# Linear-attention steps, weight splits and evictions at the block ends of the projection in a hybrid decoder step

## The reference, cut to what matters

```python
h = rms_norm(x, g_norm)
z = einsum('btd,dn->btn', h, w_in)              # all mixers' inputs and gates
ya = fox_attention(...) * silu(ga)              # forgetting attention
a_logit = einsum('btr,rk->btk', lrb, w_gla_up) + b_gla
log_a = log_sigmoid(a_logit) / GLA_TAU
ob, gla_new = gla_chunked(qb, kb, vb, log_a, gla_state)   # gated linear attention
yb = rms_norm(ob, g_gla) * silu(gb)
yc = bc * short_conv(cc * xc) * silu(gc)
merged = sum over the three of sigmoid(mg[i]) * (y_i @ w_branch_i)
out = x + merged @ w_out;  y = rms_norm(out, g_final)
```

## Time and profile before

| | us |
|---|---|
| Median of 3 executions (4195.01 to 4203.75) | 4199.2 |
| The profiled execution's own time | 4200.65 |
| Its span | 4198.8 |
| PE busy in the span | 3777.5 (90%) |
| DVE, ACT, POOL busy | 1787.0, 1705.8, 1082.0 |
| PE idle before L895, ended by DVE prj_att | 68.4 (11 times) |

### The profile page before, as it was taken

How to read it: one execution, slowest core, us unless ns; L and a number is a source line. 1 busy time by engine, 2 the same in 40 slices (tenths; PEclk the granted TensorE clock), 3 DMA queues, 4 the chain that set the end, 5 groups by cost and what they waited for, 6 DMA issues and landing times. The chain is left out here.

```text
span 4198.8 us, 60616 instructions
## 1 busy us (share of the span) xinstructions
PE 3777.5 (90%) x19285; PEld 3081.9 (73%) x19285; DVE 1787.0 (43%) x2968; ACT 1705.8 (41%) x3497; POOL 1082.0 (26%) x927
## 2 busy tenths in 40 slices
PE   7999999989999989996999993799898999599999
PEld 6787777767777778775877873577777777378887
DVE  3233433222134433232434443576666666554432
ACT  3224423435224424432443441466666666131222
POOL 0011222120011221211000000166666666622200
PEclk9999999999999999997999996899999999699999
DMA  4233333233233233324010002688888888454422
GB/s 142 92 106 110 116 131 128 87 112 116 90 110 116 98 132 130 117 82 123 1 41 11 1 11 66 211 290 287 279 283 276 289 292 277 147 214 166 157 105 82
DMA packets 356189, 590.18 MB, mean 141 GB/s; under 512 B 44953, under 2 KB 91137, under 8 KB 355974
## 3 DMA queue, kind: packets, MB, share of 16 engines
q1 hardware_dynamic: 349998, 580.21, 41.3%
q10 hardware_dynamic: 5408, 5.12, 0.4%
q0 software_dynamic: 576, 2.10, 0.2%
HBM read 475.38 MB, written 111.97 MB: 140 GB/s over the span
## 5 line engine op out<-in xcount | busy, mean ns | idle before, releaser
L854 PE MATMUL prj_z_ps<-prj_w_hi,prj_h_hi 128*128 128x512 f32 x2312 | 937.7, 406 | 15.3 <-DMA prj_bias_b<-in_b_gla_dram 9.4
L855 PE MATMUL prj_z_ps<-prj_w_lo,prj_h_hi 128*128 128x512 f32 x2312 | 913.2, 395 | 0.0
L856 PE MATMUL prj_z_ps<-prj_w_hi,prj_h_lo 128*128 128x512 f32 x2312 | 913.1, 395 | 0.0
L1800 POOL TENSOR_TENSOR sa_v_lo<-sa_v_raw,sa_v_hi 128x1024 fp32r<-128x1024 f32 x256 | 603.7, 2381 | 379.2 <-DVE sa_v_hi L1956 379.2
L854 PEld LDWEIGHTS prj_z_ps<-prj_w_hi,prj_h_hi 128*128 128x128 f32 x2312 | 443.8, 192 | 106.5 <-DVE prj_w_lo L678 9.9
L856 PEld LDWEIGHTS prj_z_ps<-prj_w_hi,prj_h_lo 128*128 128x128 f32 x2312 | 441.6, 191 | 96.7
L855 PEld LDWEIGHTS prj_z_ps<-prj_w_lo,prj_h_hi 128*128 128x128 f32 x2312 | 443.0, 192 | 87.1
L1944 DVE TENSOR_TENSOR sa_kT_lo<-sa_t_ps,sa_kT_hi 128x512 fp32r<-128x512 f32 x512 | 352.1, 690 | 252.5 <-ACT sa_kT_hi L1832 249.4
L1832 ACT CAST sa_kT_hi<-sa_t_ps 128x512 fp32r<-128x512 f32 x512 | 297.3, 584 | 239.0 <-PE sa_t_ps L2036 183.9
L678 DVE TENSOR_TENSOR prj_w_lo<-prj_w_raw,prj_w_hi 128x512 fp32r<-128x512 f32 x274 | 187.3, 703 | 408.6 <-ACT prj_w_hi L556 407.9
L2036 PE MATMUL sa_t_ps<-sa_ident,sa_k_raw 128*128 128x128 f32 x2048 | 305.8, 285 | 55.0 <-DVE sa_kT_lo L1944 54.1
(11 more groups left out here) (303 smaller groups left out, 6029.1 us busy)
## 6 DMA issues: line engine op xcount, KB each, us to landing
sa_k_raw<-in_cache_k_dram SPq DMA_DIRECT2D x512, 256.0 KB, 3.7
sa_v_raw<-in_cache_v_dram SPq DMA_DIRECT2D x512, 256.0 KB, 4.1
prj_w_raw<-in_w_main_dram SPq DMA_DIRECT2D x272, 256.0 KB, 3.2
z_scratch<-prj_z_sb SPq DMA_DIRECT2D x272, 256.0 KB
mo_mg<-z_scratch SPq DMA_DIRECT2D x51, 512.0 KB, 4.4
prj_cu<-extp_scratch SPq DMA_DIRECT2D x48, 256.0 KB
pa_raw<-z_scratch SPq DMA_DIRECT2D x12, 1024.0 KB, 10.9
prj_x_in<-in_x_all_dram SPq DMA_DIRECT2D x17, 512.0 KB, 3.8
```

The lines of the kernel that those rows point to most:

```text
L854: pe.matmul(out, h_hi[:, slot_of(t), k], hi, start=(k == 0), stop=False)
L855: pe.matmul(out, h_hi[:, slot_of(t), k], lo, start=False, stop=False)
L856: mm = pe.matmul(out, h_lo[:, slot_of(t), k], hi, start=False, stop=(k == KC - 1))
L1800: pool.tensor_tensor(v_lo[:, slot, part], v_raw[:, slot, part], v_hi[:, slot, part].bitcast(F32), ALU.subtract).then_inc(vlo_ready, 1)
```

## The change

At a block end ACT and DVE now run `gla_steps(u)` first, then all eight splits; `evict(u)` is put off to the next unit, behind that unit's `gla_steps`. SP issues the eight loads of a block end before the unit's store. There are six raw buffers in place of four; to make room, `junk` (the unused output of the square) becomes bf16. The waits for the gates' weights (`up_loaded`) and for DVE's zero fills move from before the first unit to the linear attention's own steps.

```diff
-    W_RING, RAW, Z_RING, PS_RING = 9, 4, 4, 3
+    W_RING, RAW, Z_RING, PS_RING = 9, 6, 4, 3
-        junk = m.sb("junk", [P, D_MODEL])
+        junk = m.sb("junk", [P, D_MODEL], BF16)
 # SP, at every unit
-                for s in BEFORE.get(u, []):
+                for s in BEFORE.get(u, []) + AFTER.get(u, []):
                     load_w(s + RAW)
                 store(u)
-                for s in AFTER.get(u, []):
-                    load_w(s + RAW)
 # ACT, gla step 1
+                    act.wait_ge(up_loaded, 32)
+                    act.wait_ge(gla_filled, GLA_FILLED)
 # ACT, before the units
-            act.wait_ge(up_loaded, 32)
-            act.wait_ge(gla_filled, GLA_FILLED)
 # ACT and DVE, at every unit
-                if u not in BLOCK_ENDS:
-                    gla_steps(u)
-                for s in BEFORE.get(u, []):
-                    split(s)
-                evict(u)
-                for s in AFTER.get(u, []):
-                    split(s)
+                gla_steps(u)
+                if u - 1 in BLOCK_ENDS:
+                    evict(u - 1)
                 if u in BLOCK_ENDS:
-                    gla_steps(u)
+                    for s in BEFORE.get(u, []) + AFTER.get(u, []):
+                        split(s)
+                else:
+                    evict(u)
 # ACT and DVE, after the last unit
+            evict(len(UNITS) - 1)
 # PE: gla step 0, and before the units
+                    pe.wait_ge(up_loaded, 32)
-            pe.wait_ge(up_loaded, 32)
```

## The result

The changed kernel takes 4048.6 us (median of 4, 4047.0 to 4052.3) against 4200.6 beside it: a ratio of 0.9644, 95% interval 0.9632 to 0.9656. The profiled execution's span is 4048.1 us, 150.7 less than before. The forecast was 4068 with a range from 4048 to 4120: the sign and the mechanism were right, and the gain came out 19 us larger than the sum.

The account below looks back on a forecast made before the run. PE, busy for 90% of the span, was taken to set the time. The sum -97.9 - 34 + 10 - 4 - 6 = -131.9 us from 4200.65 gave 4068.8 for the profiled execution, stated as 4068, range 4048 to 4120.

Parts of the forecast that it names:

- gla_steps first: At block ends in the projection, the linear attention's step ahead of the splits removes five lines of PE waits: 97.9 us.
- Half clock: Behind 17 PE waits in the projection, stretches at the 1.2 GHz level go, 2.0 us each: 34 us.
- The cost of splits behind the step: Splits and `keep` run later at 27 block ends, 0.4 us each: 10 us back, bounds 0 and 40.
- the scale: Times counted from the start of a block's last unit as 0; PE asks for the next unit's `keep` at 11.8.
- Six raw buffers: At block ends, two extra buffers make the new order fit, margin 0.7 us; with four the fifth slice comes late.
- Eviction put off, at no cost: At block ends, the eviction comes 5 to 6 us later, before PE needs that PSUM buffer: nothing.
- Slices late on SP's account: Where SP is late in the projection, PE's waits for `w_lo` shrink: 4 us taken, bounds 0 and 5.9.
- Start: At the kernel's start, gate weights awaited later let PE begin sooner: 6 us taken, bounds 2 and 9.4.
- junk in bf16: ACT's square with bf16 output, with ACT's own waits: between 0 and 1 us either way, taken as 0.

Follow-up runs that it names:

- Experiment 1: The changed kernel with the old block-end order and SP's order put back, six raw buffers and late gate waits kept: 4144.4 us, ratio 0.9865.
- experiment 5: The kernel before with only `keep` moved ahead of the splits at block ends, all else as it was: 4128.2 us, ratio 0.9827.
- experiment 7: The changed kernel with POOL's convolution products and sums cut to 16 of 512 columns (wrong values): 4041.6 us in a single execution.
- experiment 2: The changed kernel with four raw buffers in place of six: 4078.2 us, ratio 0.9711.
- experiment 6: The changed kernel with the eviction back between seventh and eighth split and SP's eighth load behind the store: 4056.3 us, ratio 0.9654.
- experiment 4: The kernel before with matmuls nobody reads added at 13 block ends to keep PE busy in its waits: 4183.1 us, ratio 0.9961.

## Why the prediction was right, point by point

- *gla_steps first*: 97.9 us forecast, 97.3 gone. Experiment 1 shows it by undoing it. The reading "PE waits for `keep`, `keep` waits in DVE's queue" is shown by experiment 5, which moves `keep` alone. The prediction said that `keep` was late only because of what stands ahead of it; part of its lateness was that the splits ahead of it themselves waited for raw slices, and experiment 1 prices that at 28 us of the 97.9.
- *Half clock*: forecast 17 x 2.0 = 34 us from one window, measured 39.3 by the 2 us windows. This term was sized too small: the 17 slow stretches run from 3.1 to 5.8 us behind their waits, 4.4 on average, and half of their lengths makes 37. The other 2 us or so stand behind two waits for `prj_w_lo` of 2.0 and 1.8 us, which the sum did not give a clock term. PE's drawn busy time fell by 43.5, 4.2 more than the clock's part. The 23 waits fewer (33 to 10), each with some 0.16 us hidden behind a matmul drawn too long, would make 3.7 of it, an estimate.
- *The cost of splits behind the step* was the larger miss: 10 us forecast, 0.6 us of `keep` measured, and the rest inside the 2.7 of `prj_w_lo`. At the end of block GC the scale was right to half a microsecond for DVE's step and splits, and a microsecond too late for `keep` (11.1 with landings, 10.1 measured). The landings in fact got longer (median 3.9, longest 6.7 us, in place of 3.2 and 5.4); yet the waits did not come. On the prediction's own scale a landing of 3.9 puts `keep` at 11.8, just when PE asks, so the median was still early enough. POOL had been charged with up to 1.0 us for eight splits; the convolution's part is 0.4 on average (experiment 7). Why the longest landings cost nothing is not shown.
- *Six raw buffers*: the sum said that four would not fit; experiment 2 shows 15.8 us of waits for slices and 28 to 30 us in all. It named the fifth slice as the late one, and the waits came at the sixth to eighth. What it did not say is that six would help the old order as well (experiment 1).
- *Eviction put off, at no cost*: no row shows a PSUM wait. It had been costed as free, and together with SP's loads ahead of the store it is worth about 9 us (experiment 6).
- *Slices late on SP's account*: 4 forecast, 5.9 became 2.7, so 3.2.
- *Start*: 6 forecast, 5.6 measured, with the wait for the fourth x tile near 31 us that the sum contained (29.6 to 32.3). That the two agree so closely is luck: over the traces with either start the gain lies between 4.6 and 9.0 us.
- *junk in bf16*: taken as 0, and the square on ACT takes 1.06 us as before; no run changes it alone.
- Not in the sum: 4.1 us of small waits in the same stretch that went too, and 2.3 us that the later stages took back without a change of theirs.
- *The range*: with every small term at its best bound the sum is -97.9 - 34 - 5.9 - 9.4 = -147.2, or 4053.5 us for the profiled execution, which took 4049.8. The half clock had no range of its own. The last 5 us above the lower end of 4048 came from no term, and the measured time lies there: that it is inside the range is luck.

The measured parts are 97.3 + 43.5 + 3.2 + 4.1 + 5.6 = 153.7, against 153.0 between the two starts of the forget-gate stage.

## What to carry to other kernels

When an engine waits at a seam of the schedule, ask what stands in the releaser's queue ahead of the small operation it waits for: moving one operation of 0.4 us ahead of the splits gave 73 us here, and with six buffers in place the order of the whole step and the eviction is worth 96. Then work out the next margin on the same scale, buffer by buffer, because the wait moves on to the next unit if the rest of the queue stays as it is. Price the slow clock behind each wait from all of the waits, not from one, and use idle rows as a lower bound where operations are drawn longer than their spacing.

## What the runs showed of the hardware

TensorE's half clock behind a wait could be priced by itself: 292 matmuls that nobody reads, 66 us of work at 0.23 us each, made the kernel 15 us faster, because they kept the granted clock up until the real work came (39.3 to 15.0 us lost at the low clock). In the changed kernel PE runs for 1600 us at a granted clock of 1.00 without a fall, though it waits ten times for up to 1.1 us. In experiment 4 a wait of 1.48 us was followed by half clock, and the fall came only after PE had resumed, at 1488.28 (windows as above: length, busy and records, granted clock, DMA share, GB/s):

```profile
1488.00:1490.00 2.00, 1.72 (x10) 1.50 (x11) 0.60 (x2) 0.42 (x2) 0.00 (x0) 0.91 0.75 289
1490.00:1492.00 2.00, 2.00 (x6) 1.61 (x5) 1.01 (x3) 1.90 (x6) 0.00 (x0) 0.50 0.01 2
1492.00:1494.00 2.00, 2.00 (x8) 1.52 (x8) 1.76 (x4) 0.19 (x1) 0.09 (x1) 0.74 0.00 0
```

Waits of 1.55 us at two other block ends of the same run were not followed by it. The length of a wait alone does not decide it in these traces; what else does stays open.
